# Gate block loaded and split first in the opening, two products moved behind a combination in each first group

## The reference, cut to what matters

```
def swiglu(x, w_in, w_out):
    gu = x @ w_in
    g, u = jnp.split(gu, 2, axis=-1)
    return (jax.nn.silu(g) * u) @ w_out
...
        x = x + 0.5 * swiglu(rms_norm(x, ffn1_norm[l]), ffn1_w_in[l], ffn1_w_out[l])
...
        gate, up = jnp.split(h2 @ w_gate_up[l], 2, axis=-1)
        x = x + (jax.nn.silu(gate) * up) @ w_down[l]
```

## Time and profile before

| | us |
|---|---|
| median of 3 runs | 1581.43 |
| lowest, highest | 1580.72, 1581.44 |
| the profiled execution | 1581.31 |
| its span, first to last instruction | 1579.5 |
| TensorE busy (matmuls) | 1563.9 |
| VectorE busy | 1274.1 |
| ScalarE busy | 902.0 |

### The profile page before, as it was taken

One profiled execution on the slowest core, in us unless ns is written; L12 is line 12 of the kernel. 1 busy time (PEld: TensorE's weight loads), 2 busy tenths in 40 slices (PEclk: granted clock), 3 DMA queues, 4 the chain that ended last, 5 costly groups with the idle time before them and its releaser, 6 DMA issues.

```text
span 1579.5 us, 18791 instructions
## 1 busy us (share of the span) xinstructions
PE 1563.9 (99%) x7346; PEld 1294.5 (82%) x7346; DVE 1274.1 (81%) x1181; ACT 902.0 (57%) x1000; POOL 219.9 (14%) x271
## 2 busy tenths in 40 slices
PE   8999999999999999999999999999999999999998
PEld 6888888888888888888888888888888888888886
DVE  7888856679887989875677988778898876798886
ACT  7555555646555655555565655566655556665554
POOL 1132112011000113211201000131200002110000
PEclk9999999999999999999999999999999999999999
DMA  9987665558766778766456776561877565277662
GB/s 302 279 230 219 230 210 164 185 183 248 246 196 177 241 233 248 215 223 212 156 178 211 255 237 211 161 220 54 266 231 230 191 192 172 96 260 231 192 210 91
DMA packets 182415, 327.29 MB, mean 207 GB/s; under 512 B 13028, under 2 KB 77944, under 8 KB 182328
## 3 DMA queue, kind: packets, MB, share of 16 engines
q1 hardware_dynamic: 169064, 300.66, 57.2%
q0 software_dynamic: 12960, 24.94, 8.7%
q10 hardware_dynamic: 304, 0.50, 0.1%
HBM read 322.88 MB, written 2.88 MB: 206 GB/s over the span
## 4 chain that ended last, share of the span: by engine, by line
PE 92%; DVE 3%; ACT 2%; issue 1%; DMA 1%; SPq 0%; POOLq 0%; POOL 0%; ACTq 0%; DVEq 0%
PE pg L2263 19%; PE pg L2265 19%; PE pg L2264 19%; PE acc L2263 9%; PE acc L2265 9%; PE acc L2264 9%; PE pg L2384 2%; ACT whi L1100 1%; PE pg L2276 1%; DVE wlo L1616 1%; DVE work L1641 1%; DMA raw<-in_ffn_w_in 1%; PE acc L2557 0%; PE acc L2539 0%; PE acc L2728 0%
## 5 line engine op out<-in xcount | busy, mean ns | idle before, releaser
L2263 PE MATMUL pg<-whi,xTh 128*128 128x512 f32 (+1 forms) x1096 | 436.2, 398 | 4.2 <-DVE wlo L1616 2.5
L2265 PE MATMUL pg<-whi,xTl 128*128 128x512 f32 (+1 forms) x1096 | 426.5, 389 | 0.0
L2264 PE MATMUL pg<-wlo,xTh 128*128 128x512 f32 (+1 forms) x1096 | 425.7, 388 | 0.0
L1616 DVE TENSOR_TENSOR wlo<-raw,whi 128x2048 fp32r<-128x2048 f32 x143 | 328.8, 2299 | 52.4 <-ACT whi L1100 48.7
L1100 ACT ACTIVATE whi<-raw 128x2048 fp32r<-128x2048 f32 x143 | 274.1, 1917 | 153.7 <-PE pg L2265 99.4
L1516 DVE TENSOR_TENSOR wlo<-raw,whi 128x2048 fp32r<-128x2048 f32 (+1 forms) x87 | 198.5, 2282 | 59.4 <-ACT whi L1012 59.2
L2263 PEld LDWEIGHTS pg<-whi,xTh 128*128 128x128 f32 x1096 | 205.9, 188 | 48.9 <-DVE wlo L1616 3.0
L2265 PEld LDWEIGHTS pg<-whi,xTl 128*128 128x128 f32 x1096 | 205.7, 188 | 42.5
L2264 PEld LDWEIGHTS pg<-wlo,xTh 128*128 128x128 f32 x1096 | 206.1, 188 | 40.0 <-issue 1.0
L1616 DVE TENSOR_TENSOR wlo<-work,whi 128x2048 fp32r<-128x2048 f32 x90 | 208.2, 2313 | 31.4 <-ACT whi L1100 31.4
L2263 PE MATMUL acc<-whi,bTh 128*128 128x512 f32 (+1 forms) x572 | 227.2, 397 | 0.0
(11 more groups left out here) (276 smaller groups left out, 1962.0 us busy)
## 6 DMA issues: line engine op xcount, KB each, us to landing
raw<-in_ffn_w_in SPq DMA_DIRECT2D x124, 512.0 KB, 5.6
raw<-in_ffn_w_out SPq DMA_DIRECT2D x88, 512.0 KB, 4.5
raw<-in_mix_w_in SPq DMA_DIRECT2D x64, 512.0 KB, 4.7
raw<-in_w_gate_up SPq DMA_DIRECT2D x64, 512.0 KB, 5.4
work<-in_ffn_w_in SPq DMA_DIRECT2D x48, 512.0 KB, 5.8
raw<-in_w_down SPq DMA_DIRECT2D x44, 512.0 KB, 4.4
work<-in_ffn_w_in POOLq DMA_DIRECT2D x24, 512.0 KB, 8.5
raw<-in_w_in SPq DMA_DIRECT2D x24, 512.0 KB, 5.4
```

What stands on the lines that cost most here:

```text
L1616: v.tensor_tensor(wlo[:, u % SLOTS, :], source, f32(whi[:, u % SLOTS, :]), ALU.subtract).then_inc(s.w_lo_ready, 1)
L2263: pe.matmul(dst, xh, wh, start=first and i == 0, stop=False, skip_group_check=onto)
L2264: pe.matmul(dst, xh, wl, start=False, stop=False, skip_group_check=onto)
L2265: mm = pe.matmul(dst, xl, wh, start=False, stop=last and i == len(pairs) - 1, skip_group_check=onto)
```

## The change

It has two parts. In the opening (first FFN stage, first group), SyncE issues the first gate block ahead of the first up block; VectorE makes the low part of that gate block (unit 4) ahead of `first_sum(0)`; and since the end of a split then no longer says that the sum has read `raw`, SyncE waits for the sum before it loads the second gate block (unit 8) into that slot. In the first group of every FFN stage, `product(2, 0)` and `product(2, 1)` move from behind `third_sum` to behind `combine_w`.

```diff
@@ sync engine, ffn @@
                     if rnd == 0 and i == 0:
                         sp.wait_ge(raw_landed[0], 64)
-                    up_block(i, 0, up_k0)
-                    gate_block(i, 0)
+                        gate_block(i, 0)
+                        up_block(i, 0, up_k0)
+                    else:
+                        up_block(i, 0, up_k0)
+                        gate_block(i, 0)
...
                     plain(2 + i, 1)
+                    if rnd == 0 and i == 0:
+                        sp.wait_ge(s.w_sum_ready, T1_AT)
                     gate_block(i, 1)
@@ vector engine, ffn @@
                 form_lo_part(1)
-                first_sum(0)
+                if start:
+                    loaded_lo(SUM_UNITS[0][0])
+                    first_sum(0)
+                else:
+                    first_sum(0)
+                    loaded_lo(SUM_UNITS[0][0])
                 for i in range(GROUPS):
                     qa, qb = PLAIN_UNITS[2 + i]
-                    loaded_lo(SUM_UNITS[i][0])
                     if i == 0:
                         product_lo(0)
+                    else:
+                        loaded_lo(SUM_UNITS[i][0])
...
                         third_sum(i)
-                        product(2 + i, 0)
                     else:
                         third_sum(i)
                         product(2 + i, 0)
...
                     if i:
                         product_lo(3 * i)
-                    product(2 + i, 1)
+                        product(2 + i, 1)
                     combine_u(i)
                     summed_lo(i, 4)
                     if i:
                         product_lo(3 * i + 1)
                     combine_w(i)
+                    if i == 0:
+                        product(2, 0)
+                        product(2, 1)
                     loaded_lo(DOWN_UNITS[3 * i + 1])
```

## The result

The changed kernel takes 1585.18 us (median of 11 runs, 1583.99 to 1586.77), before 1581.43 (11 runs in the same series, 1580.51 to 1581.81). The ratio is 1.0025, 95% interval 1.0016 to 1.0034. The kernel became 3.75 us slower. The forecast was 1584.2 with a range of 1581.2 to 1585.6, so the time lies inside, 1.0 above the forecast. The profiled execution took 1584.75 us with a span of 1582.9 us.

The account below looks back on a forecast made before the run. TensorE, busy 1563.9 of 1579.5 us, was taken as the bound. Opening 1.39 plus six groups 1.4 made 2.8, so 1581.43 became 1584.2; the sum's own range was 1583.3 to 1584.9, the outer range 1581.2 to 1585.6.

Parts of the forecast that it names:

- The step that VectorE stands still until ScalarE has converted unit 4: Opening: VectorE idles from 29.89 to 31.28, making everything behind it 1.39 us later.
- the gain at the first pause is lost in the second: Opening: TensorE's first pause ends 0.81 earlier, but late products lengthen the second; together 3.11 before, 4.50 after.
- signs of being wrong: Opening: wrong if ScalarE starts converting before 29.3 or the second pause ends by 38.1; or `combine_w` vanishes from TensorE's waits.
- the group's price: First group of six FFN stages: 0.12 lateness plus 0.11 restart, 0.23 us each, 1.4 together; bounds 0 and 0.35.
- `combine_w` doesn't come earlier: Group: unit 11's split still waits for ScalarE until 60.92, idle 1.38 instead of 0.60; gain nothing.
- the lateness of `down(1)`: Group: unit 12's split ends at 66.79, so TensorE goes on at 66.85 instead of 66.73, 0.12 late.
- The small wait of `acc` for `wlo`: Group: sign expected in the profile after, a new TensorE wait, six times 0.1 us or less.
- the load would stay hidden, at 0.12 each: Group: alternative by the Trainium skill's rule on weight loads pulled ahead; each pause costs 0.12, the six 0.7.
- the first (the six waits shrink): Group: TensorE's six `combine_w` waits shrink by up to 0.77 each, 4.6 in all, giving 1578.2; chance 0.08.
- the second (the products are free): Group: products behind `combine_w` are free or restart costs less, giving 1582.8 to 1583.5; chance 0.15.
- the third: Opening: first pause shrinks by 0.81 and the second doesn't grow; with the six at 1.4, 1582.0; chance 0.05.
- the fourth: Dearer: six groups at 0.35, opening 1.5 or more through unit 8's late load; 1585.0, up to 1586; chance 0.12.

Follow-up runs that it names:

- The earlier conversion: Kernel before plus the change's opening part, with ScalarE also converting unit 4 ahead of form parts 2 and 3: 1582.31 us against 1581.38.
- the filled pauses: Kernel before plus the change's opening part, with 5 and 9 unused matmuls in TensorE's two opening pauses: 1582.10 us against 1581.45.
- the load order: Kernel before with only SyncE's first gate block loaded ahead of the first up block: 1581.55 us against 1581.54.
- the opening alone: Kernel before with only the change's SyncE part and first VectorE part, products where they were: 1583.89 us against 1581.38.
- its filled version: Whole changed kernel plus 5 and 9 unused matmuls in TensorE's two opening pauses: 1584.07 us against 1581.54 for the kernel before.
- `third_sum` early: Kernel before with `third_sum` moved ahead of the split of unit 9 in each first group: 1576.34 us against 1581.38.
- one product moved: Kernel before with only `product(2, 1)` behind `combine_w`, `product(2, 0)` staying: 1581.70 us against 1581.45.
- the products alone: Kernel before with both products of each first group behind `combine_w`, opening as before: 1583.33 us against 1581.38.
- the three filled kernels: Unused matmuls in TensorE's opening pauses, added to: opening part alone (1582.10 us), whole change (1584.07), kernel before with `third_sum` ahead of unit 9's split (1575.92).

## Why the prediction was right, and where it fell short

**The opening.** The step that VectorE stands still until ScalarE has converted unit 4 was right: 1.39 forecast, 1.38 in the trace, and without clock losses 1.1 to 1.2 in the times (1582.10 and 1582.24 against 1581.05). That the gain at the first pause is lost in the second was right as well (forecast 33.6 and 39.4; measured 33.3 and 39.1 with the arrival 0.3 earlier). The earlier conversion and the filled pauses showed the cause, and the load order and SyncE's wait were rightly priced at nothing. One of the prediction's signs of being wrong did appear: ScalarE started the conversion at 29.02, before 29.3. It doesn't count against the step, since VectorE and TensorE came there 0.3 earlier as well; the sign should have been put relative to the form parts.

**What the sum left out.** It had no term for the clock, and this is the step that was missing. The text ahead of the prediction read a granted clock of 0.999 off one execution, and the prediction took it for all. By their mean clock 52 of the 75 runs of before in the experiments (15 of 27, 19 of 27, 18 of 21) already had a stretch at the lower level in the opening, at some 0.6 us each, hidden in part by the wait behind it. The change moved the idle time: the long pause is now the second, and no wait close behind it takes up the loss. With the opening alone a run that meets it loses 1.8. Against its filled version the changed kernel loses 1.1, and the kernel before some 0.4 (1581.43 against the 1581.05 of its runs at 0.999). The difference, 0.7, would be the larger part of the 1.0 us by which the forecast was low; the group's price gives another 0.6, and by the times, though not by the trace, the opening came out 0.2 to 0.3 cheaper. This split isn't firm. The changed kernel's own runs at 0.999 have the median 1584.63, which is 0.55 below the median of all and 0.56 above its filled version. By them the clock explains only 0.2 of the 1.0, and the 0.5 between the two is open. That the clock costs something is shown, and 0.2 to 0.7 of the 1.0 is what these runs allow.

**The group.** That `combine_w` doesn't come earlier, and why, was right, and `third_sum` early proved it. The price was mis-sized: 0.23 a group forecast, 0.27 to 0.34 in the trace and 1.95 / 6 = 0.33 in the times. The term that failed is the lateness of `down(1)`, in the first stage's rows 0.21 (67.77 to 67.98) rather than 0.12. I took 0.06 from the end of the split to the matmul; here it was 0.14 (67.84 to 67.98), the weight load standing at 67.95. The extra spacing was 0.08 rather than 0.11. It stayed inside the bounds of 0 and 0.35. The small wait of `acc` for `wlo`, which the prediction wanted to see six times, is in no wait row; the loss stands only in the starts and in the gap of 0.45 ahead of the weight load. That the load would stay hidden, at 0.12 each, didn't come about: it stands at 67.95, behind the 67.93 at which the matmul ahead ends. With one product moved the operand was just in time, the load stood at 66.60 under the matmul of 66.58, and nothing was lost.

**The chances.** Slower by over 0.2% had 0.30 and "within" 0.64; measured was 0.25%, over that bound at its middle and across it in its interval (0.16 to 0.34%). With 0.7 more for the clock the forecast would have been 1584.9, on the other side of the bound of 1584.6. Of the rivals, the first (the six waits shrink), the second (the products are free) and the third fell. Of the fourth, the group at 0.33 is close to its 0.35, but the opening wasn't dearer and unit 8 wasn't late. The time of 1585.18 lies above 1584.9, where the prediction's range for its own sum ends. That it is inside the outer range is in part luck: the room up there was made for a later load and a dearer opening, and the clock filled it.

## What to carry to other kernels

Before moving work ahead of a wait, look at what the waited-for operation itself waited for: if it had been idle behind another engine, taking work from ahead of it only lengthens that idle time, and what pays is to move the producer of the other engine's input, here one line for 5 us. Work moved behind it costs when the next thing that the bounding engine wants comes after it and has less margin than the work is long, so count that margin in the trace first. And when two executions differ by more than the sum explains, compare the spread of the runs and their mean granted clock before looking for another stall.

## What the hardware showed that I had not expected

One pause of 2.54 or 2.77 us on TensorE was enough in more than half of the runs (by their mean clock 52 of 75 before, 7 of 11 of the opening alone) for the granted clock to drop to 0.50, with matmuls 0.43 us apart instead of 0.23. In the traces the drop came 0.6 us behind the end of the pause of 2.54 (the products alone) and about 1.1 us behind that of 2.77 (the opening alone); the same pauses in the profiled runs of the kernel before and of the changed kernel brought none. With the idle time cut to 0.4 to 0.7 us each by unused matmuls, none of 27 runs of the three filled kernels had a lower mean clock than 0.999. What the drop costs depends on the next wait: 0.6 us in the kernel before, 1.8 in the opening alone, where none follows soon.
